# Spreading the first half's inverse roots with two wide rounded products

## The reference

```
hn = x * rsqrt(mean(x*x) + 1e-6) * norm_g          # per token
a, b, gate = split(hn @ w_in)                      # three times 1024 channels
u = a * sigmoid(b)
u = causal depthwise convolution of u, 31 taps, + conv_b
u = LayerNorm(u) * ln_g + ln_b                     # per token, over channels
y = silu(u) * silu(gate)
out = x + y @ w_out
```

## Time and profile before

| what | value |
|---|---|
| median of 3 runs | 354.79 us (354.25 to 354.96) |
| the profiled execution | 354.75 us |
| its span in the profile | 352.9 us |
| TensorE busy | 348.6 us, 99% |
| VectorE busy | 325.0 us, 92% |
| ScalarE busy | 229.7 us, 65% |
| GpSimd busy | 267.2 us, 76% |
| granted TensorE clock | 1.0 of full speed |

### The profile page before, as it was taken

The page is one execution under the profiler, slowest core; times in us unless marked ns, Lnnn a source line. Parts: engine busy times, 40 slices in busy tenths (PEclk is TensorE's granted clock), DMA queues, the critical chain, the costliest instruction groups (busy, mean ns, idle before and its releaser), DMA issues.

```text
span 352.9 us, 4764 instructions
## 1 busy us (share of the span) xinstructions
PE 348.6 (99%) x1564; PEld 289.6 (82%) x1564; DVE 325.0 (92%) x520; ACT 229.7 (65%) x330; POOL 267.2 (76%) x192
## 2 busy tenths in 40 slices
PE   8999999999999999999999999999999999999996
PEld 8888888888888888888888888888888888878786
DVE  5679799999999999989999998998799999999972
ACT  6889685567936870998669777975574872443400
POOL 0129999999999999789999999896695551359240
PEclk9999999999999999999999999999999999999999
DMA  8995011211410321404110410441733398047152
GB/s 276 414 412 206 27 61 59 79 42 59 119 61 8 93 81 59 119 2 119 59 60 3 119 59 12 109 119 60 238 121 120 119 390 326 0 139 237 44 207 90
DMA packets 30520, 43.51 MB, mean 123 GB/s; under 512 B 18336, under 2 KB 18848, under 8 KB 30496
## 3 DMA queue, kind: packets, MB, share of 16 engines
q1 hardware_dynamic: 30352, 43.21, 35.9%
q10 hardware_dynamic: 144, 0.00, 0.0%
HBM read 34.82 MB, written 4.19 MB: 111 GB/s over the span
## 4 chain that ended last, share of the span: by engine, by line
PE 92%; DVE 6%; issue 1%; DVEq 0%
PE mm L655 68%; PE acc L731 9%; PE mm L672 6%; PE mm L731 6%; DVE sgate L1280 2%; DVE x_lo L1260 2%; DVE nat L1292 2%; PE acc L777 1%; PE acc L712 1%; PE acc L722 1%; PE acc L649 0%; PE acc L643 0%; PE acc L645 0%; DVE ones L1083 0%; DVEq L1278 0%
## 5 line engine op out<-in xcount | busy, mean ns | idle before, releaser
L655 PE MATMUL mm<-x_hi,w_hi 128*128 128x512 f32 x352 | 137.4, 390 | 0.0
L655 PE MATMUL mm<-x_hi,w_lo 128*128 128x512 f32 x352 | 137.0, 389 | 0.0
L655 PE MATMUL mm<-x_lo,w_hi 128*128 128x512 f32 x352 | 136.9, 389 | 0.0
L1192 DVE SCALAR_TENSOR_TENSOR acc<-u,chan,acc 128x512 f32<-128x512 f32 x157 | 110.5, 748 | 0.1
L1514 POOL TENSOR_TENSOR pconv<-pconv,prod 128x512 f32<-128x512 f32 x60 | 77.0, 1306 | 1.3 <-ACT prod L886 1.3
L655 PEld LDWEIGHTS mm<-x_lo,w_hi 128*128 128x128 f32 x352 | 66.1, 188 | 13.7
L655 PEld LDWEIGHTS mm<-x_hi,w_lo 128*128 128x128 f32 x352 | 66.1, 188 | 13.7
L655 PEld LDWEIGHTS mm<-x_hi,w_hi 128*128 128x128 f32 x352 | 66.1, 188 | 13.6
L1192 DVE SCALAR_TENSOR_TENSOR acc<-u,w_sum,acc 128x512 f32<-128x512 f32 x90 | 67.3, 747 | 2.4 <-ACT acc L868 2.3
L886 ACT ACTIVATE prod<-u,chan 128x512 f32<-128x512 f32 x69 | 47.9, 716 | 19.8 <-POOL pconv L1514 18.4
L1458 POOL TENSOR_TENSOR w_lo<-raw,w_hi 128x1024 fp32r<-128x1024 f32 (+1 forms) x21 | 49.7, 2365 | 7.8 <-ACT w_hi L835 7.8
(11 more groups left out here) (111 smaller groups left out, 528.2 us busy)
## 6 DMA issues: line engine op xcount, KB each, us to landing
raw<-w_in SPq DMA_DIRECT2D x22, 512.0 KB, 3.3
nat<-x_t SPq DMA_DIRECT2D x16, 256.0 KB, 5.4
sgate<-x SPq DMA_DIRECT2D x8, 512.0 KB, 10.4
raw<-w_out SPq DMA_DIRECT2D x8, 512.0 KB, 3.2
nat<-x SPq DMA_DIRECT2D x8, 512.0 KB, 8.3
y<-nat SPq DMA_DIRECT2D x15, 256.0 KB, 2.1
raw_late<-w_out SPq DMA_DIRECT2D x4, 512.0 KB, 4.5
sig<-w_out SPq DMA_DIRECT2D x4, 512.0 KB, 4.1
```

The source lines that it names most:

```text
L655: ins = nc.tensor.matmul(bank(("unit", m, h)), w[:, m % 3, k, :], xx[:, k, half(h)], start=(k == 0 and i == 0), stop=(k == KC - 1 and i == 2))
L1192: ins = nc.vector.scalar_tensor_tensor(dst, chain_in(j, chain, k), tap(j, chain, k), chain_bank(j, chain), ALU.mult, ALU.add)
```

## The change

Half 0's roots are now spread as half 1's are: by two wide matmuls over rounded high and low diagonals in `diags`. They are made differently. GpSimd rounds the column of roots itself (`rms_hi`) and subtracts to get the low column (`rms_lo`), in a new function `split_rms` behind each of the two `inverse_rms` of half 0. ScalarE multiplies the identity with the root, rounded on writing, for the high diagonal, and with the low root for the low diagonal: eight activations in place of four, in the order high 0 to 2, low 0 to 2, high 3, low 3. ScalarE first waits for half 1's spread, since both use `diags`. The spread moves one block later, before block 3. The two new columns are taken out of a gap in SBUF.

```diff
-SPREAD_AT = {1: (0, 4), 0: (3, 0, 2)}
+SPREAD_AT = {1: (0, 4), 0: (3, 0, 3)}
...
-        sb("gap_before_w", [P, 96])
+        rms_hi = sb("rms_hi", [P, TPH], F32R)
+        rms_lo = sb("rms_lo", [P, TPH])
+        sb("gap_before_w", [P, 80])
...
             def spread_rms(h):
 
+                spread = rms_spread(h).rearrange("p (t q) -> p t q", t=TPH)
                 if h == 1:
-                    spread = rms_spread(1).rearrange("p (t q) -> p t q", t=TPH)
                     pe.wait_ge(ones_r_ready, 1)
-                    pe.wait_ge(diag_hi_ready, TPH)
-                    nc.tensor.matmul(spread, ones_r[:], diags[:, 0, :, :], start=True, stop=False)
-                    pe.wait_ge(diag_lo_ready, TPH)
-                    ins = nc.tensor.matmul(spread, ones_r[:], diags[:, 1, :, :], start=False, stop=True)
-                else:
-                    for i in range(TPH):
-                        pe.wait_ge(diag_ready, i + 1)
-                        ins = nc.tensor.matmul(rms_spread(0)[:, i * P:(i + 1) * P], ones[:], diag(i), start=True, stop=True)
-                ins.then_inc(rms_all_ready, 1)
+                pe.wait_ge(diag_hi_ready if h == 1 else first_hi_ready, TPH)
+                nc.tensor.matmul(spread, ones_r[:], diags[:, 0, :, :], start=True, stop=False)
+                pe.wait_ge(diag_lo_ready if h == 1 else first_lo_ready, TPH)
+                nc.tensor.matmul(spread, ones_r[:], diags[:, 1, :, :], start=False, stop=True).then_inc(rms_all_ready, 1)
...
-            def rms_diagonal(t):
+            def rms_diagonals(tiles):
 
                 act.wait_ge(ident_in, 16)
-                act.wait_ge(rms_ready, rms_count(t))
-                nc.scalar.activation(diag(t), ident[:], ACT.Copy, scale=rms[:, t:t + 1]).then_inc(diag_ready, 1)
+                act.wait_ge(rms_all_ready, 1)
+                act.wait_ge(rms_ready, rms_count(tiles[-1]))
+                for t in tiles:
+                    nc.scalar.activation(diags[:, 0, t, :], ident[:], ACT.Copy,
+                                         scale=rms[:, t:t + 1]).then_inc(first_hi_ready, 1)
+                act.wait_ge(rms_lo_ready, 2 if TPH - 1 in tiles else 1)
+                for t in tiles:
+                    nc.scalar.activation(diags[:, 1, t, :], ident[:], ACT.Copy,
+                                         scale=rms_lo[:, t:t + 1]).then_inc(first_lo_ready, 1)
...
-            for t in range(TPH):
-                rms_diagonal(t)
+            rms_diagonals(range(TPH - 1))
+            rms_diagonals((TPH - 1,))
...
+            def split_rms(tiles):
+
+                part = slice(tiles[0], tiles[-1] + 1)
+                n = 2 if TPH - 1 in tiles else 1
+                pool.wait_ge(rms_ready, rms_count(tiles[0]))
+                nc.gpsimd.tensor_scalar(rms_hi[:, part], rms[:, part], 1.0, None, ALU.mult).then_inc(rms_hi_ready, 1)
+                pool.wait_ge(rms_hi_ready, n)
+                nc.gpsimd.tensor_tensor(rms_lo[:, part], rms[:, part], rms_hi[:, part].bitcast(F32),
+                                        ALU.subtract).then_inc(rms_lo_ready, 1)
...
-            inverse_rms(range(TPH - 1))
-            inverse_rms((TPH - 1,))
+            for tiles in (range(TPH - 1), (TPH - 1,)):
+                inverse_rms(tiles)
+                split_rms(tiles)
```

More of the change, by code:

```diff
@@ L199, in gated_conv_layer @@
         ones_r_ready = sem("ones_r_ready")
-        diag_ready = sem("diag_ready")
+        first_hi_ready = sem("first_hi_ready")
+        first_lo_ready = sem("first_lo_ready")
+        rms_hi_ready = sem("rms_hi_ready")
+        rms_lo_ready = sem("rms_lo_ready")
         diag_hi_ready = sem("diag_hi_ready")
@@ L465, in half @@
             return slice(h * HALF, (h + 1) * HALF)
-        def diag(i):
-            return sgate[:, i, 0:P]
         def words(columns):
```

## The result

| | before | after |
|---|---|---|
| median of the runs taken together | 354.68 us (10 runs, 354.25 to 355.12) | 356.62 us (10 runs, 355.45 to 357.38) |
| the profiled execution | 354.75 us, span 352.9 | 356.37 us, span 354.6 |

The ratio of after to before is 1.0048, interval 1.0039 to 1.0058: the changed kernel is slower by 1.4 to 2.1 us. The forecast was 355.5 in 354.3 to 356.2, so the direction had the probability of 0.48 and the size was beyond the range. I follow the profiled execution, which is 1.62 us longer, and ask of each row of the prediction where its part of the 1.62 entered.

A forecast was written before the change was run, and what follows sets the result against it. The prediction took a chain of GpSimd, ScalarE, VectorE, then TensorE to set the end. GpSimd's +1.0 - 0.16 - 0.1 = +0.75 on 354.75 gave 355.5 us, TensorE's -0.46 being off the path; range 354.3 to 356.2.

The forecast's parts named there:

- What bounds the kernel: Chain to the end: GpSimd from 31 to 140 us, ScalarE to 153, VectorE to 328.6, then TensorE.
- 0.85 was written: Delay passed from GpSimd's queue at 43 us through ScalarE to VectorE: 1.0 less a gap of 0.16.
- 0.46 predicted: TensorE's spread with two wide products in place of eight records: 0.46 us saved, lost in waits at 272.5 and 328.6.
- one of 1.2 was expected: Sign of a right forecast: a new TensorE wait of about 1.2 us at 273, the start of the output products.
- rival: Other outcomes: delay absorbed 0.16, TensorE's saving passes 0.06, small operations dear 0.09, tail falls differently 0.04, late diagonals 0.02.
- GpSimd's four instructions: Root splitting on GpSimd: 1.12 us start to start, charged as 1.0, bounds 0.56 and 1.7.
- the term of 0.75: GpSimd's net delay on the path to the end: +1.0 - 0.16 - 0.1 = +0.75 us.
- No transfer is added or moved: DMA traffic: nothing charged; SyncE's queue is late by as much, with transfers wanted much later.
- ScalarE's diagonals in front of TensorE: Eight diagonals done by 35.65, TensorE wanting them at 36.04 and 36.27: 0.6 us of cover, no stall charged.
- The roundings of ScalarE for GpSimd's next subtractions stay ahead of it: ScalarE, 1.2 us late behind the diagonals, would not delay GpSimd, since GpSimd is later too; nothing charged.
- By 153.5 that is nothing, because it waits 1.14 us there anyway: VectorE starting 0.3 us later at 37.45 is absorbed by its wait for ScalarE's first tap; nothing charged.
- the 0.3 that was written: ScalarE's copy of the spread, behind diagonals and two roundings, was to start 0.3 us later.

The follow-up runs named there:

- e1: The kernel before with only GpSimd's four new instructions added, their results unread: 355.72 us, ratio 1.0032.
- h3: The changed kernel with 14 warm-up products in place of 11, 12 TensorE instructions more: 355.88 us, ratio 1.0024.
- h4: The kernel before with four more diagonals on ScalarE, unread, and nothing else: 355.56 us, ratio 1.002.
- e3: The kernel before with the exact float spread one block (0.68 us) later and nothing else: 355.05 us, ratio 1.0015.
- e2: The changed kernel with the high and low parts of the roots computed by VectorE instead of GpSimd: 356.10 us, ratio 1.0044.
- g1: The changed kernel with three of GpSimd's low halves made by VectorE and ScalarE rounding unit 4's weights ahead of a sigmoid: 356.29 us, ratio 1.005.
- h1: The changed kernel with half 0's high and low diagonals made by VectorE, nothing new on GpSimd or ScalarE: 358.34 us, ratio 1.0095.
- h2: The changed kernel with VectorE making the diagonals and one more low half, and ScalarE's roundings ahead of the spread's copy: 356.91 us, ratio 1.0064.
- f2: The kernel before with 8 warm-up products in place of 11, 12 TensorE instructions fewer: 354.97 us, ratio 1.0006.
- g2: The kernel before with three of GpSimd's low halves made by VectorE and ScalarE rounding unit 4's weights ahead of a sigmoid: 354.71 us, ratio 0.9996.
- f1: The changed kernel with 24 already satisfied waits (12 instructions) put ahead of TensorE's warm-ups: 356.06 us, ratio 1.0038.
- e4: The changed kernel with GpSimd's four new instructions made twice, the second result unread: 357.00 us, ratio 1.0069.

## Why the prediction was wrong in size

**What bounds the kernel: right.** The chain GpSimd, ScalarE, VectorE, TensorE carried the delay: 1.24 at 44 us, 1.29 at 142, 1.28 at 221, 1.28 at 246.75, each with the 0.30 of the late start in it, so about 1.0 where 0.85 was written. TensorE's 0.42 us of saving (0.46 predicted) is in its new waits, 0.9 and 0.8 us of them where one of 1.2 was expected. No rival came true.

**GpSimd's four instructions: right in mechanism, mis-sized.** "I take 0.19: ... Four instructions from start to start: 4 x 0.28 = 1.12 us" became 1.21 where, with the overlap, 1.0 was charged. The small subtraction took 0.19, as taken. The rounding that takes the stall ended 0.10 us behind VectorE's wide subtraction (33.76 against 33.66), not 0.05, and what follows the one-column rounding starts 0.32 behind it, not 0.28. In e1, where the four are alone, the end moved by 0.71 in the profile, against 0.75 in the sum, but by 1.17 in the medians (0.7 to 1.6). The 0.71 is a favourable execution, so the term of 0.75 was probably 0.3 to 0.4 too small.

**"No transfer is added or moved": the step that failed.** No transfer of the program was added, but a fetch of its instructions moved. It came 2.6 us later, for a part at least because TensorE's program was 12 instructions shorter, and fell on the weight load ahead of the last DMA transposition. In the profile this is the 0.62 us between planes and statistics; in the medians, h3, in which the fetch is out of the way and the rest of the change stays, is 0.74 us faster than the changed kernel. At h3's 355.88 the forecast would have been inside its range, 0.4 above its centre; these 0.4 are the mis-sized term above. I had looked for the saving of TensorE to be worthless; that it could be harmful was not among the rivals.

**ScalarE's diagonals in front of TensorE: right, with less cover than said.** The last low diagonal is this row of ScalarE's:

```profile
35.59 0.40 ACT L813 ACTIVATE diags<-ident,rms_lo 128x128 fp32r<-128x128 f32 x1
```

It ends at 35.99, 0.14 us ahead of the product that reads it (36.13), where "0.6 us of cover is left" was written; TensorE shows no wait there.

**ScalarE's diagonals in front of GpSimd: "The roundings of ScalarE for GpSimd's next subtractions stay ahead of it" was false reasoning that left the sum right.** In the changed kernel GpSimd doesn't wait for them, but only because it is late by as much. Alone they cost 0.75 us (h4 against the kernel before of its call, 355.56 - 354.81), against 1.17 for GpSimd's; the intervals overlap (0.4 to 1.0 and 0.7 to 1.6), and the two profiled executions are alike (355.47 and 355.46).

**The later spread: "By 153.5 that is nothing, because it waits 1.14 us there anyway" was wrong as well.** I followed the copy into VectorE only, not back through the gates and ScalarE's rounding of the next weights to GpSimd's queue. Alone it costs 0.5 us (e3 against its kernel before, 355.05 - 354.55). In the changed kernel the copy came at 36.94, 0.49 later than before; 0.30 of that is the late start, so the 0.3 that was written held up to there.

The three delays don't add. GpSimd's 1.2, ScalarE's 1.2 and the later spread's all arrive at GpSimd at 43 to 44 us, and the end sees the longest. That is why costing two of them at nothing did little harm to the sum: GpSimd's four alone cost 1.17, the whole change with the fetch clear 1.07. It is also why e2 and g1, which relieved GpSimd, didn't help. h1 and h2 took GpSimd's and ScalarE's part away together and lost more by diagonals that came late.

**What stays open.** The changed kernel's runs spread from 355.45 to 357.38, those of the kernel before from 354.25 to 355.12; part of that may be the start of GpSimd's work, 31.5 to 32.2 over the traces, and part where the fetch falls, but neither was measured run by run. A profiled execution can't say how often the fetch hits, and the price of a hit differs: 0.7 to 0.9 us between h3 and the changed kernel, not told from nothing in f2. In the kernel before TensorE's spread of the means was as late as VectorE's statistics and would cover a part of a late transposition; that f2 loses less than the changed kernel fits that, but it is argued only. The lag of 4.1 to 4.7 goes with the time for which packets were held, 0.76 to 1.33; what sets that time isn't known. Where the half of the 2.6 us comes from that f2 doesn't show isn't either. No variant here beats the kernel before; g2 equals it.

## What to carry to other kernels

Where a change shortens one engine's program, look in the DMA part for the fetches of instructions, and at what transfer that someone waits for lies 1 to 3 us behind each: the fetch can shift onto it, or onto the load queued ahead of it. Before an edit is costed at nothing because its engine "stays ahead", work out the case in which its neighbour isn't late; where several paths of like length enter one queue, all must be shortened before it shows. Idle time of VectorE beside GpSimd's wide subtractions isn't idle: small operations put there took four times as long (h1, 0.28 to 0.35 became 1.25 to 1.30).

## What the runs showed of the hardware

- A fetch of 0.02 MB on the instruction queue, from 0.7 us ahead to 1.2 us behind the split of the planes, went with a weight load that landed 4.8 to 5.4 us after its issue (3.1 to 3.9 otherwise) and a DMA transposition behind it that arrived 0.7 to 1.3 us later (lag 3.40 against 4.10 to 4.73), fourteen traces out of fourteen on their side. The transposition's held packets ended just ahead of the load's landing each time.

- Already satisfied waits aren't free on TensorE: with 24 of them the first warm-up came 1.30 us later (f1, 2.34 against 1.04) and the first product 1.17 us later (6.92 against 5.75).

- GpSimd's small operations on 1 to 3 columns took 0.19 to 0.23 us, the powers aside, and followed each other at 0.28 to 0.32, whether they had one input or two; in e4 the added roundings, which wait for nothing, started 0.15 to 0.16 behind the operation before them. Beside a wide VectorE subtraction, one with one input took 0.53 and 0.72.
